# Scores of 16 attention maps as two rounded products, high and low parts stacked in the partitions

## The reference, cut to what matters

```python
# second layer, 256 tokens, head dimension 64
sc = einsum('qd,kd->qk', q, k) * 64 ** -0.5 - slope * (tq - tk)   # float32
p  = masked_softmax(sc)                                           # causal; swa: 128 tokens, with a sink
o  = p @ v
# moba: q = mq, k = mk, 4 heads, each with its own keys
# nsa:  q = nq, 4 heads over ONE key head, three branches: compressed keys (15 of them), slc, win
# diff: two maps per head, of 32 dimensions each (df1, df2), own keys
# swa:  q = sq, 4 heads over 2 key heads
```

## Time and profile before

| | |
|---|---|
| time, median of 3 runs | 961.27 us (960.97 to 962.59) |
| the profiled execution | 961.01 us |
| its span, first to last instruction | 959.2 us |
| TensorE busy | 939.3 us (98%) |
| VectorE, ScalarE, GpSimd busy | 619.1, 426.5, 259.0 us |
| maps segment, about | 560 to 672 us of the span |

### The profile page before, as it was taken

One profiled execution on the slowest core, in us unless ns is written; L12 is line 12 of the kernel. 1 busy time (PEld: TensorE's weight loads), 2 busy tenths in 40 slices (PEclk: granted clock), 3 DMA queues, 4 the chain that ended last, 5 costly groups with the idle time before them and its releaser, 6 DMA issues.

```text
span 959.2 us, 16689 instructions
## 1 busy us (share of the span) xinstructions
PE 939.3 (98%) x6806; PEld 874.3 (91%) x6806; DVE 619.1 (65%) x1169; ACT 426.5 (44%) x814; POOL 259.0 (27%) x136
## 2 busy tenths in 40 slices
PE   8999999999999989999999999999999999999997
PEld 8879999878999879999999789998899999999996
DVE  6635887558556778435443666776878676766584
ACT  6433313563543574332334654774734333242422
POOL 3322203330010144333334435312233131231320
PEclk9999999999999999999999999999999999999999
DMA  8535332242433556554554353322546555555521
GB/s 311 188 132 192 116 117 105 88 154 89 138 117 139 185 192 219 215 180 176 191 205 176 132 187 133 122 88 99 188 172 223 177 198 195 178 191 187 193 88 44
DMA packets 23499, 154.02 MB, mean 161 GB/s; under 512 B 2800, under 2 KB 3568, under 8 KB 5888
## 3 DMA queue, kind: packets, MB, share of 16 engines
q1 hardware_dynamic: 22704, 150.80, 43.9%
q0 software_dynamic: 576, 2.10, 0.7%
q10 hardware_dynamic: 144, 0.07, 0.0%
HBM read 151.38 MB, written 1.05 MB: 159 GB/s over the span
## 4 chain that ended last, share of the span: by engine, by line
PE 91%; DVE 4%; ACT 3%; issue 1%; DMA 0%; DVEq 0%; ACTq 0%
PE pb L496 90%; PE pb L499 2%; DVE FA L505 1%; ACT FA L502 1%; DVE wl L505 1%; ACT wh L502 1%; ACT R L502 1%; DVE R L511 1%; DVE X L511 0%; ACT L502 0%; DMA FA<-in_meta 0%; ACT st L502 0%; DVE FA L508 0%; DVE FA L526 0%; DVE st L523 0%
## 5 line engine op out<-in xcount | busy, mean ns | idle before, releaser
L496 PE MATMUL pb<-R,wh 128*128 128x256 f32 (+1 forms) x3024 | 555.7, 285 | 5.3 <-ACT R L502 1.7
L496 PEld LDWEIGHTS pb<-R,wh 128*128 128x128 f32 x3024 | 472.0, 190 | 15.4 <-ACT R L502 3.2
L496 PE MATMUL pb<-R,wl 128*128 128x256 f32 (+1 forms) x1512 | 423.7, 282 | 0.0
L505 POOL TENSOR_TENSOR wl<-raw,wh 128x1024 fp32r<-128x1024 f32 (+1 forms) x94 | 228.0, 2430 | 626.8 <-ACT wh L502 462.8
L505 DVE TENSOR_TENSOR wl<-raw,wh 128x1024 fp32r<-128x1024 f32 (+1 forms) x184 | 235.4, 1290 | 101.7 <-ACT wh L502 99.6
L496 PEld LDWEIGHTS pb<-R,wl 128*128 128x128 f32 x1512 | 286.7, 190 | 0.0
L502 ACT ACTIVATE wh<-raw 128x1024 fp32r<-128x1024 f32 (+1 forms) x212 | 218.7, 1047 | 109.9 <-PE pb L496 108.8
L496 PE MATMUL pb<-wh,R 128*128 128x512 f32 (+2 forms) x724 | 234.9, 389 | 4.1 <-DVE FA L520 1.5
L496 PEld LDWEIGHTS pb<-wh,R 128*128 128x128 f32 (+1 forms) x724 | 134.5, 186 | 35.8 <-DVE FA L520 1.7
L496 PE MATMUL pb<-wl,R 128*128 128x512 f32 (+2 forms) x372 | 144.3, 388 | 0.0
L502 ACT ACTIVATE FA<-pb 128x256 f32<-128x256 f32 (+7 forms) x151 | 65.4, 442 | 135.7 <-PE pb L496 115.5
(11 more groups left out here) (120 smaller groups left out, 504.8 us busy)
## 6 DMA issues: line engine op xcount, KB each, us to landing
raw<-in_w SPq DMA_DIRECT2D x137, 1024.0 KB, 4.8
X<-in_x SPq DMA_DIRECT2D x2, 512.0 KB, 4.2
raw<-in_w SPq DMA_DIRECT2D x2, 512.0 KB, 6.4
post<-in_ffn_post SPq DMA_DIRECT2D x2, 512.0 KB, 5.7
post<-in_w POOLq DMA_DIRECT2D x2, 512.0 KB, 4.7
FA<-in_w POOLq DMA_DIRECT2D x2, 512.0 KB, 6.0
out<-X SPq DMA_DIRECT2D x4, 256.0 KB, 2.0
cst<-in_cst SPq DMA_DIRECT2D x1, 799.0 KB, 12.1
```

Source lines behind the costliest of these rows:

```text
L496: return self.real.matmul(*a, **k) if self.real else self
L505: return self.real.tensor_tensor(*a, **k) if self.real else self
```

## The change

The 16 maps of moba, slc, win and swa get float32r operands. A query head is one tile of 128 partitions: the 64 rows that ScalarE copies are the rounded high part, the other 64 rows are the low part, which VectorE writes as PSUM minus high part. They lie in `R3`, in the place where `join` of the same pair writes afterwards. For the keys there are two tiles, `KH` with the high part in both halves and `KL` with the low part in both halves. ScalarE writes the head's own half of `KH`, VectorE that of `KL`, and SyncE copies each to the other half. So there are four transfers for each of four pairs of keys (slc with win, the two swa, moba 0 with 1, moba 2 with 3), 16 where there were 8, and every one of the 16 maps waits for its four. A score is two accumulated products in each of two passes, over 128 keys for the first queries and over 256 for the second. `cmp_score` becomes 16 float32r products over 128 partitions and 16 columns.

```diff
                     for c in range(2):
                         nk = 128 + 128 * c
                         b = bank(("score", m_, c), B5)
-                        for k0 in range(0, nk, 128):
-                            m = e.matmul(b[:, k0:k0 + 128], M["q"][:, 128 * c:128 * c + 128], M["k"][:, k0:k0 + 128], start=True,
-                                         stop=True)
+                        q = M["q"][:, 128 * c:128 * c + 128]
+                        if "apart" in M:
+                            for k0 in range(0, nk, 128):
+                                m = e.matmul(b[:, k0:k0 + 128], q, M["k"][:, k0:k0 + 128], start=True, stop=True)
+                        else:
+                            e.matmul(b[:, 0:nk], q, KH[M["k"]][:, 0:nk], start=True, stop=False)
+                            m = e.matmul(b[:, 0:nk], q, KL[M["k"]][:, 0:nk], start=False, stop=True)
                         m.then_inc(*pe.up(("score", m_, c)))
...
                 elif kind == "cmp_score":
                     e.wait_ge(*act.at("cmp_kv"))
+                    e.wait_ge(*dve.at("cmp_kv"))
                     e.wait_ge(*act.at(("evac", "nq", 1)))
+                    e.wait_ge(*dve.at(("evac", "nq", 1)))
                     for par in range(2):
                         b = bank(("cmp_score", par), B5)
-                        r = slice(64 * par, 64 * par + 64)
                         for x in range(4):
                             c, hp = divmod(x, 2)
-                            m = e.matmul(b[:, 16 * x:16 * x + 15], nq[r, hp, 128 * c:128 * c + 128], kcT[r, :], start=True, stop=True)
+                            q = QH(2 + hp, par)[:, 128 * c:128 * c + 128]
+                            e.matmul(b[:, 16 * x:16 * x + 16], q, KCH, start=True, stop=False)
+                            m = e.matmul(b[:, 16 * x:16 * x + 16], q, KCL, start=False, stop=True)
```

ScalarE's part of the `evac` steps of queries and keys:

```diff
-                    elif name == "mk" or step == ("evac", "s", 2):
+                    elif use[1:] in QUERY:
                         e.wait_ge(*pe.at(use))
-                        for i in range(2):
-                            e.activation(KEY["moba", 2 * n + i] if name == "mk" else KEY["swa", i, i], b[:, 0:256], ACT.Identity,
-                                         scale=rows(i)).then_inc(*act.up(step))
+                        for i, (p, _) in enumerate(SIDES):
+                            e.activation(QH(QUERY[use[1:]], i)[p, :], b[p, 0:256], ACT.Copy).then_inc(*act.up(step))
+                        banks.ended(use, act.now())
+                    elif use[1:] in PAIRS:
+                        e.wait_ge(*pe.at(use))
+                        for k, (p, _) in zip(PAIRS[use[1:]], SIDES):
+                            e.activation(KH[k][p, :], b[p, 0:256], ACT.Copy).then_inc(*act.up(step))
                         banks.ended(use, act.now())
```

VectorE's part, which is new (the keys of `tm2_out` get the same subtraction), and SyncE's transfers:

```diff
+                    elif use[1:] in QUERY:
+                        e.wait_ge(*act.at(step))
+                        for i, (p, other) in enumerate(SIDES):
+                            q = QH(QUERY[use[1:]], i)
+                            e.tensor_tensor(q[other, :], b[p, 0:256], rf(q[p, :]), ALU.subtract).then_inc(*dve.up(step))
+                        banks.ended(use, dve.now())
+                    elif use[1:] in PAIRS:
+                        e.wait_ge(*act.at(step))
+                        for k, (p, _) in zip(PAIRS[use[1:]], SIDES):
+                            e.tensor_tensor(KL[k][p, :], b[p, 0:256], rf(KH[k][p, :]), ALU.subtract).then_inc(*dve.up(step))
+                        banks.ended(use, dve.now())
...
-            def moved(dst, src, sig):
-
-                e.dma_start(dst[64:128, :], src[0:64, :]).then_inc(*sig.up("all", by=16))
-                e.dma_start(dst[0:64, :], src[64:128, :]).then_inc(*sig.up("all", by=16))
+            def again(t):
+
+                for k, (p, other) in zip(PAIRS[t], SIDES):
+                    for x in (KH[k], KL[k]):
+                        e.dma_start(rf(x[other, :]), rf(x[p, :])).then_inc(*in_keys[t].up("all", by=16))
```

`MADE` and every string of `MIX` are replaced, so steps stand elsewhere in all segments, while the set of steps stays the same. Over the whole kernel the letters of `MADE` go from 141 d, 70 p, 43 v, 22 q to 145 d, 71 p, 35 v, 25 q; for the 18 units split in the maps segment they go from 4 d, 6 p, 5 v, 3 q to 7 d, 9 p, 2 v, none q. The maps string before and after:

```diff
-    "maps": "...a.....a.ddbabe.dae.cg.gef.f..bcgfgfa.gc.ea.cefgc.ahheaeach.fehd.edibechff.gbg.iijmihjik.c.amc"
-            "oko.cl.jiobdlb.jjhihibmdqknbcnkbkbpdqonedodpnlndcoqmepikq.i.lpqilpm.mq.",
+    "maps": "......c.da...db.cadcedegcgac.gfbf.ecaagbeaeg.c.def.hfgd.hef.aggec.fiiaiihejeiah.bb.bdjffh.d.i.ba"
+            "mh...mnbciicnck.bbhhjdmnddoblkkeoqpcemklmkqi.jpqloj.nnpooilqpqpli.qkmo.",
```

More of the change, by code:

```diff
@@ L568, in program @@
         WL = [sb(f"wl{i}", 1024, FR) for i in range(NBASE)]
-        with nc.sbuf_tensor("keys", [128, 2 * 8 * T1], FP) as keys:
+        with nc.sbuf_tensor("keys_r", [128, 9 * 256], FR) as keys_r, nc.sbuf_tensor("keys", [128, 8 * 256], FP) as keys:
             pass
@@ L580, in program @@
         with nc.sbuf_tensor("FA", [128, NFA], FP) as FA:
+            pass
+        with nc.sbuf_tensor("keys_f", [128, 7 * 256 + 32], FR) as keys_f:
             pass
@@ L712, in program @@
         o = 0
-        mq = fa(o, 512).rearrange("p (n t) -> p n t", n=2); o += 512
-        more = [fa(o + 256 * i, 256) for i in range(3)]; o += 768
+        o += 7 * 256 + 32
         TM1 = fa(o, 1024).rearrange("p (c n) -> p c n", c=2); o += 1024
@@ L724, in program @@
         o += 480
[L725 removed]
+        hk = fa(o, 30); vc = fa(o + 48, 64, 15); o += 112
         hr = fa(o, 128, 30); o += 128
@@ L736, in program, with QH @@
         assert o <= NFA, o
-        PROJ = {("mq", n): mq[:, n, :] for n in range(2)} | {("nkc", 0): nkc} | {("nq", n): nq[:, n, :] for n in range(2)} \
-            | {("d", n): dqk[:, n, :] for n in range(4)} | {("s", n): sqk[:, n, :] for n in range(2)}
+        PROJ = {("nkc", 0): nkc} | {("d", n): dqk[:, n, :] for n in range(4)}
         cols = (slice(0, 128), slice(128, 384))
-        names = [("moba", h) for h in range(4)] + [(m, i) for m in ("slc", "win") for i in range(2)] \
-            + [("swa", n, i) for n in range(2) for i in range(2)] + [("df", h, i) for h in range(4) for i in range(2)]
-        KEY = dict(zip(names, [keys[:, 256 * i:256 * i + 256] for i in range(17)] + more))
+        KEY = {("df", h, i): keys[:, 512 * h + 256 * i:512 * h + 256 * i + 256] for h in range(4) for i in range(2)}
+        names = [("slc",), ("win",)] + [(m, i) for m, n in (("swa", 2), ("moba", 4)) for i in range(n)]
+        tiles = [keys_r[:, 256 * i:256 * i + 256] for i in range(9)] + [keys_f[:, 256 * i:256 * i + 256] for i in range(7)]
+        KH, KL = dict(zip(names, tiles[0::2])), dict(zip(names, tiles[1::2]))
+        KCH, KCL = keys_f[:, 1792:1808], keys_f[:, 1808:1824]
+        PAIRS = {"tm2": names[0:2], ("s", 2): names[2:4], ("mk", 0): names[4:6], ("mk", 1): names[6:8]}
+        def QH(kt, i):
+            return R3[:, 512 * kt + 256 * i:512 * kt + 256 * i + 256]
+        QUERY = {("nq", n): 2 + n for n in range(2)} | {("s", n): 6 + n for n in range(2)} | {("mq", n): n for n in range(2)}
+        LOWER, UPPER = slice(0, 64), slice(64, 128)
+        SIDES = ((LOWER, UPPER), (UPPER, LOWER))
         def rows(i):
@@ L751, in program @@
         for h in range(4):
[L752 to L753 removed]
+            n = h // 2
+            MAPS["moba", h] = dict(q=QH(n, h % 2), k=("moba", h), of=("evac", "mq", n), bias=(0, h),
                                    scale=0.125, v=[TM1[:, c, 64 * h:64 * h + 64] for c in range(2)], vs="tm1_out")
[L755 to L757 removed]
+            for m, gi, voff in (("slc", 1, 0), ("win", 2, 64)):
+                MAPS[m, h] = dict(q=QH(2 + n, h % 2), k=(m,), of=("evac", "nq", n),
                                   bias=(1, h), scale=0.125, v=[TM2[:, c, voff:voff + 64] for c in range(2)], vs="tm2_out",
@@ L1457, in scalar @@
                     e.wait_ge(*pe.at("tm2"))
-                    for i, m in enumerate(("slc", "win")):
-                        e.activation(KEY[m, i], banks.of(("tm2", 2))[:, 0:256], ACT.Identity,
-                                     scale=rows(i)).then_inc(*act.up(("tm2_out", "k")))
+                    for k, (p, _) in zip(PAIRS["tm2"], SIDES):
+                        e.activation(KH[k][p, :], banks.of(("tm2", 2))[p, 0:256], ACT.Copy).then_inc(*act.up(("tm2_out", "k")))
                     banks.ended(("tm2", 2), act.now())
@@ L1922, in vector @@
                     banks.ended(("tm2", 1), dve.now())
+                    b = banks.of(("tm2", 2))
+                    e.wait_ge(*act.at(("tm2_out", "k")))
+                    for k, (p, _) in zip(PAIRS["tm2"], SIDES):
+                        e.tensor_tensor(KL[k][p, :], b[p, 0:256], rf(KH[k][p, :]), ALU.subtract).then_inc(*dve.up(("tm2_out", "k")))
+                    banks.ended(("tm2", 2), dve.now())
                     e.wait_ge(*act.at("tm2_out"))
@@ L2045, in vector @@
                     banks.ended("cmp_hid", dve.now())
+                elif kind == "cmp_kv":
+                    b = banks.of(step)
+                    e.memset(rf(KCH[:, 15:16]), 0.0).then_inc(*dve.up())
+                    e.memset(rf(KCL[:, 15:16]), 0.0).then_inc(*dve.up())
```

(13 more changed lines are left out.)

45 lines of the change are left out of this document (22 added, 23 removed).

## The result

The changed kernel takes 963.44 us (median of 7 runs, 963.23 to 965.5) against 961.12 before (7 runs): a ratio of 1.0027, 95% interval 1.0015 to 1.0038. It is slower, by 2.3 us, where I had forecast 2.4 us less; the time lies 1 us above my range. Its span is 961.7 us, 2.5 more than before.

A forecast was written before the change was run, and what follows sets the result against it. TensorE's work was taken to bound the maps segment. 961.0 - 3.2 (scores) + 0.3 (cmp_score) + 0.1 (other engines) + 0.4 (transfers) = 958.6 us, or 958.9 against the median 961.3; range 956.4 to 962.4.

The forecast's parts named there:

- What bounds: Maps segment, 556 to 672 us: TensorE's work is the time, so removed products save one for one unless new waits arise.
- The disputed price: Maps' scores: a float32r instruction with 128 moving columns costs 0.115 us; the 16 maps save 3.2 us.
- cmp_score 1.8 forecast: cmp_score: 16 instructions at 0.11 us take 1.8 us instead of 1.46, 0.3 more.
- Rivals 1 and 3: Maps' 128-column float32r: as dear as float32, 0.22 us, chance 0.14; or loading faster, 0.06 to 0.08 us, chance 0.08.
- The other engines' added work: Maps segment: VectorE gets 8.4 us of subtractions, ScalarE 1.6 us of copies, splits shift between them; 0.1 us allowed for waiting.
- the hidden 8 to 12 us: Maps segment: VectorE's and ScalarE's work stays covered by TensorE unless an in-order queue stands still at the wrong place.
- The transfers: Moba's scores wait for four copies: 5.2 us needed, 5.5 and 6.0 us of cover, 0.4 us of waiting.
- the last subtraction 0.42: Moba's key copies: VectorE's final subtraction adds 0.42 us to the 5.2 us from key product to landing.
- The clock: Stretch from 672 to 700 us: the granted clock is 0.94 while TensorE waits on chains, and stays unchanged.
- Steps placed anew: Segments far from the maps: the new order changes 0 us, kept at -1.5 to +1.5.
- Rival 2: Moba's scores: a slab issued just before delays the copies, 3.1 and 2.6 us of waiting; no change or slower; chance 0.17.

The follow-up runs named there:

- x5: x2 with moba 0's score some 2.6 us of TensorE work later, its exponential and turn moved along; 956.91 us, ratio 0.9957 to the kernel before.
- x7: x5 with 256 instead of 128 columns moving for the first queries in both new products; 958.09 us, ratio 0.9962 to the kernel before.
- x2: The changed kernel with unit 173's low part made by VectorE instead of GpSimd; 957.48 us, ratio 0.9949 to the kernel before.
- x3: The changed kernel with 28 useless 256-column products in front of moba 0's wait for its copies; 958.98 us, ratio 0.9972 to the kernel before.
- x4: The kernel before, with its float32 scores and copies, given the new order strings MADE and MIX; 958.54 us, ratio 0.9970 to the kernel before.
- x8: The changed kernel with the old order strings MADE and MIX, keeping the new scores; 994.12 us, ratio 1.0336 to the kernel before.
- x9: x2 with the copies of high parts issued before waiting for VectorE's low parts; 955.57 us, ratio 0.9944 to the kernel before.
- x10: The changed kernel with the copies of high parts issued before waiting for VectorE's low parts; 962.09 us, ratio 1.0001 to the kernel before.
- x6: The changed kernel with moba 0's score some 4 us later, and its exponential and turn later too; 964.92 us, ratio 1.0033 to the kernel before.
- x12: x6 with unit 175's low part made by VectorE instead of GpSimd; 964.46 us, ratio 1.0027 to the kernel before.
- x1: The changed kernel with moba 0's score and exponential some 4 us of TensorE work later; 965.52 us, ratio 1.0036 to the kernel before.

## Why the prediction was wrong, by its own steps

- **What bounds, and that removed products come off one for one:** right, with the sign that I had put to it only in passing: as long as nothing makes TensorE wait.
- **The disputed price, 0.115 us for 128 columns:** right (0.46 us a map, and x5 beside x7). cmp_score 1.8 forecast, 1.79 measured. Rivals 1 and 3 are out.
- **The other engines' added work:** the durations were right (ScalarE 0.38, VectorE 0.42 and 0.43 us). "The cover holds; the hidden 8 to 12 us would appear only if an in-order queue stood still at the wrong place" named the risk and gave it no price. The sum of VectorE's work in the segment was the wrong view; its queue at 623 us was the right one.
- **The transfers, the step that failed.** I reckoned 5.2 us from the end of a product for keys to the landing, against 6.0 of cover behind mk 0, and 0.4 us of waiting. Issue spacing and landing were as reckoned. But "the last subtraction 0.42" was wrong twice. VectorE waits for both of ScalarE's writes and then makes two subtractions, 0.87 us: 0.4 more. And the term supposed that VectorE was free, while it came 3.6 us late: 1.1 for the rest of a unit, 0.1 for a reciprocal, 2.4 beside GpSimd. 5.2 + 0.4 + 3.6 is 9.2 us, and 9.4 were measured (622.99 to 632.36); less the cover that is the wait of 3.3 us. x2 takes the stand beside GpSimd away and leaves 1.0. I had allowed for ScalarE's queue and not for VectorE's.
- **The clock, priced at nothing.** "It stays as it is" looked at the one stretch where TensorE waits on chains anyway. There it costs little: the runs of the kernel before with a mean clock of 0.999 or 1.000 have 960.6 to 961.5 us, those with 0.997 have 961.0 to 961.8 but for one of 962.5. In a full stretch it costs 4.5 us (x3), more than the wait that brings it on. This term, left out, is larger than all the others.
- **Steps placed anew, taken as 0:** wrong. x4 gains 2.9 us by the order with the old scores, and the new scores are 31 us slower in the old order (x8 against the changed kernel).
- **Rival 2** had the place and the sign (copies late at moba's scores, slower) and the wrong cause, a slab ahead on the queues, and so a price of 2.6 to 2.8 us for one late group; with the clock it is 7.8. It had 0.06 of the chances for slower.

The sum as it was: x9, with the new scores and the new order and neither the late copies nor the fall of the clock, is 5.9 us below the kernel before (961.43). Adding 3.3 for the wait and 4.5 for the clock gives 1.9 us more than before; 2.3 are measured. Of the 5.9 the rows give 3.0 to the scores and x4 gives 2.9 to the order.

## What to carry to other kernels

Where TensorE is full, price a new wait twice: the wait itself and the work behind it at half clock; here 3.3 us of waiting cost nearly 8. When a step gets a new link on another engine, don't ask whether that engine has time in the segment; write down what stands in its queue in front of the link, and who else runs at that moment. Where a group of transfers depends on two engines, issue each part as it is ready: that took TensorE's wait from 3.3 to 1.9 us (x10) and from 1.0 to none (x9).

## What the runs showed of the hardware that I had not expected

A VectorE operation on two columns of SBUF that meets a GpSimd subtraction of 1024 columns lasts until that one ends: 2.41 us for 0.16 (after), 1.92 for 0.17 (x6), 1.57 in the kernel before. It was not only operations with two tensor inputs: those of x6 and of the kernel before are TENSOR_SCALARs with one.

The clock fell in or just after waits of TensorE of 1.5 (x6, x12), 1.9 (x10), 2.2 (x1) and 3.3 us, and did not after one of 1.0 (x2). The length of the wait alone doesn't decide. Every kernel with the new scores and the new order has one more wait, of 2.0 us at about 554, ahead of the maps. Behind it the clock fell in the profiled runs of x2, x7 and x12, for some 3.4 us, and stayed at full in the others. It set x2 back by 1.6 us against x3 (x2's trace is 0.5 us later at 536 us and 2.1 at 622), and x2's four runs lie in two pairs, at 956.2 to 956.5 and at 958.5 to 958.6 us. So differences of 1 to 2 us between two medians of a few runs say little here.
